# A two-layer diffusion step on one core: attention values in products of 512 columns, and layer 2's adaLN as a pass of its own

## The reference, cut to what matters

```python
def trunk_layer(x, cond, lp, ctx_kv, rope):
    mod = jax.nn.silu(cond) @ lp['w_ada'] + lp['b_ada']          # adaLN: (1024,) @ (1024, 6144)
    sh1, sc1, g1, sh2, sc2, g2 = jnp.split(mod[:, None, :], 6, axis=-1)
    h = rms_norm(x, lp['norm1']) * (1.0 + sc1) + sh1
    proj = h @ lp['w_in']                                        # gates, branches A, B and C
    ...
    o_lat = latent_attention(q_lat, q_pe, ckv, kpe)              # 8 heads, keys: own + 128 cached
    ...
    x = x + g1 * (merged @ lp['w_out'])
    h2 = rms_norm(x, lp['norm2']) * (1.0 + sc2) + sh2
    x = x + g2 * peer_ffn(h2, lp['peer_wq'], lp['peer_sub_keys'], lp['peer_u'], lp['peer_v'])

    # in latent_attention, per block of 128 queries:
    p = jax.nn.softmax(s, axis=-1)
    return jnp.einsum('bhqk,bkc->bqhc', p, ckv)                  # the values

    # in peer_ffn: each token picks 128 of 16384 experts (8 heads, 16 each)
    a = jax.nn.gelu(jnp.einsum('tkd,td->tk', jnp.take(u_tab, ib, axis=0), tb))
    return jnp.einsum('tk,tkd->td', gb * a, jnp.take(v_tab, ib, axis=0))
```

## Time and profile before

| | us |
|---|---|
| median of 3 runs (lowest, highest) | 5152.7 (5149.1, 5155.6) |
| the profiled execution's own time | 5154.9 |
| its span, first to last instruction | 5152.0 |

### The profile page before, as it was taken

How to read it: one execution, slowest core, us unless ns; L and a number is a source line. 1 busy time by engine, 2 the same in 40 slices (tenths; PEclk the granted TensorE clock), 3 DMA queues, 4 the chain that set the end, 5 groups by cost and what they waited for, 6 DMA issues and landing times.

```text
span 5152.0 us, 37623 instructions
## 1 busy us (share of the span) xinstructions
PE 4042.2 (78%) x11663; PEld 1906.6 (37%) x11663; DVE 3140.8 (61%) x7049; ACT 521.8 (10%) x1158; POOL 2525.1 (49%) x2570
## 2 busy tenths in 40 slices
PE   8889889893887777777788988989277777777777
PEld 4674543341323333333343545334122222222223
DVE  1155877667555665654554678766766666665553
ACT  1130320100001001000000224001000000000000
POOL 0003345403665665665565234550177676676674
PEclk9889999996998999999999989999699999999999
DMA  8536679718999998999998466993299999999997
GB/s 264 168 120 223 211 265 329 270 49 281 399 398 349 371 363 346 371 395 370 355 398 297 163 208 221 334 318 101 96 381 408 352 374 389 374 375 378 368 409 287
DMA packets 578101, 1562.80 MB, mean 303 GB/s; under 512 B 51104, under 2 KB 246256, under 8 KB 576626
## 3 DMA queue, kind: packets, MB, share of 16 engines
q0 software_dynamic: 368640, 1342.34, 68.8%
q1 hardware_dynamic: 208690, 217.90, 12.9%
q10 hardware_dynamic: 576, 0.16, 0.0%
HBM read 1557.44 MB, written 2.79 MB: 303 GB/s over the span
## 4 chain that ended last, share of the span: by engine, by line
PE 32%; DMA 31%; DVE 14%; POOL 13%; issue 7%; DVEq 2%; ACT 1%; SPq 0%; PEldq 0%; PEld 0%; POOLq 0%; ACTq 0%
DMA rows<-in_peer_u_dram,idx 15%; DMA rows<-in_peer_v_dram,idx 15%; POOL rows L2056 13%; PE ps L1213 10%; PE ps L757 5%; DVE rows L1941 4%; PE ps L1103 4%; PE ps L740 3%; DVE work L1983 2%; PE ps L767 1%; PE ps L802 1%; PE ps L1106 1%; DMA ring<-in_w_in_dram 1%; DVE work L1894 1%; PE ps L1007 1%
## 5 line engine op out<-in xcount | busy, mean ns | idle before, releaser
L1213 PE MATMUL ps<-rows,work 128*128 128x512 f32 x4096 | 2014.7, 625 | 662.3 <-DMA rows<-in_peer_v_dram,idx 616.0
L1941 DVE CUSTOM_DVE_ANT_0 rows<-rows,ps 128x1024 f32<-128x1024 f32 x1024 | 1248.7, 1220 | 1140.3 <-DMA rows<-in_peer_u_dram,idx 1129.1
L2056 POOL DMA_INDIRECT rows<-in_peer_u_dram,idx x1280 | 1252.9, 979 | 1336.7 <-DVE idx L1934 805.6
L2056 POOL DMA_INDIRECT rows<-in_peer_v_dram,idx x1280 | 1271.5, 993 | 1263.5 <-PE ps L1213 536.2
L1213 PEld LDWEIGHTS ps<-rows,work 128*128 128x128 f32 x4096 | 738.7, 196 | 1859.5 <-issue 1396.7
L757 PE MATMUL ps<-h_s,ring 128*128 128x512 f32 x1024 | 451.9, 596 | 3.8 <-DMA ring<-in_w_in_dram 3.8
L1941 DVE CUSTOM_DVE_ANT_0 rows<-rows,work 128x1024 f32<-128x1024 f32 x256 | 312.6, 1224 | 152.7 <-DMA rows<-in_peer_u_dram,idx 145.8
L2020 DVE TENSOR_SCALAR work<-cst,acts,g_w 128x128 f32<-128x128 f32 x1024 | 369.8, 363 | 37.6 <-PE ps L1213 22.6
L1983 DVE SCALAR_TENSOR_TENSOR work<-rows,acts,work 128x1024 f32<-128x1024 f32 x254 | 325.7, 1282 | 4.8
L757 PE MATMUL ps<-work,ring 128*128 128x512 f32 (+1 forms) x768 | 276.8, 515 | 59.7 <-DMA ring<-in_w_branch_c_dram 34.2
L757 PEld LDWEIGHTS ps<-h_s,ring 128*128 128x128 f32 x1024 | 196.4, 192 | 255.1 <-issue 250.4
(11 more groups left out here) (286 smaller groups left out, 3086.4 us busy)
## 6 DMA issues: line engine op xcount, KB each, us to landing
ring<-in_w_in_dram SPq DMA_DIRECT2D x72, 1024.0 KB, 11.4
ring<-in_w_ada_dram SPq DMA_DIRECT2D x48, 1024.0 KB, 7.7
ring<-in_peer_wq_dram SPq DMA_DIRECT2D x32, 1024.0 KB, 5.9
rows<-in_peer_u_dram,idx POOLq DMA_INDIRECT x1280, 7.3
rows<-in_peer_v_dram,idx POOLq DMA_INDIRECT x1280, 7.1
ring<-in_w_out_dram SPq DMA_DIRECT2D x16, 1024.0 KB, 12.2
ring<-in_tables_dram SPq DMA_DIRECT2D x10, 1024.0 KB, 8.0
ring<-in_w_branch_c_dram SPq DMA_DIRECT2D x16, 512.0 KB, 10.6
```

The lines of the kernel that those rows point to most:

```text
L1213: mm = pe.matmul(y_acc[:, cols], diag[:, e % TOPK, :], rows[:, ROWS + s, cols], start=e == 0, stop=e == EXPERTS - 1)
L1941: dve.tensor_tensor_reduce(rows[:, s, :], rows[:, s, :], tok, 1.0, 0.0, ALU.mult, ALU.add, dots[:, e:e + 1]).then_inc(rows_u_free, 1)
L2056: pool.indirect_dma_start(rows[:, slot0 + s, :], None, table, bass.IndirectOffsetOnAxis(ap=idx[:, t % 2, e:e + 1], axis=0)).then_inc(came[ ...
```

## The change

Two edits.

**adaLN.** A pass kind A is added: A0 stands ahead of P0, A1 between S0 and P1, each only the 24 products and copies. In `cuts` the steps of A1 get the slots -14 to 9, one each, and P1's remaining steps the slots 24 to 497. SyncE issues the 24 loads of w_ada ahead of the layer's parameter loads.

**Values.** The turned probabilities of a head's four query tiles are kept side by side (5 x 512), and the values of a head are 5 products of 512 columns, issued in steps 6, 10, ..., 34 right behind the scores. The probabilities have 2 buffers instead of 3. The buffer `work` grows by 640 columns.

The diff, without the shifted view offsets, the dispatch in the three `mixing` functions, and SyncE's `chunk_order` and `weights`, which move the 24 loads in the same way:

```diff
-INSTS = [INPUT, PROMPTS[0], SAMPLES[0], PROMPTS[1], SAMPLES[1]] + LASTS
+ADAS = [Inst("A", l) for l in range(LAYERS)]
+INSTS = [INPUT, ADAS[0], PROMPTS[0], SAMPLES[0], ADAS[1], PROMPTS[1], SAMPLES[1]] + LASTS
...
-VAL_LAG = 3
-STEPS = PAIRS + VAL_LAG + 2
+VAL_STEP = STILES + 2
+STEPS = PAIRS + 5
...
-        ring("params", ("turned", 0), ("turned", 1), *[("ada", n) for n in range(N_ADA)], "mod")
+        ring("params", ("turned", 0), ("turned", 1), "mod")
...
         if l + 1 < LAYERS:
-            pr = PROMPTS[l + 1]
-            steps = [(int(share * SPREAD * SAMPLE_SLOTS), place) for place, share in mix_share(pr)]
+            pr, ada = PROMPTS[l + 1], ADAS[l + 1]
+            steps = [(-PARTS + 1 + n, PLACE[ada, ("ada", n)]) for n in range(N_ADA)]
+            steps += [(N_ADA + int(share * (SPREAD * SAMPLE_SLOTS - N_ADA)), place) for place, share in mix_share(pr)]
...
+            def conditioning(i):
+                pe.wait_ge(cond_ready, 2)
+                for n in range(N_ADA):
+                    yield PLACE[i, ("ada", n)]
+                    w = arrived(i, ("ada", n))
+                    a = opened(i, ("ada", n))
+                    for k in range(KC):
+                        mm = pe.matmul(a[0:2, 0:CW], cond_t[:, 0:2, k], w[:, k, :], start=k == 0, stop=k == KC - 1)
+                    closed(i, ("ada", n), mm)
...
             for l in range(LAYERS):
+                weights(ADAS[l])
                 params(l)
...
+                    hv, past_step = divmod(m - VAL_STEP, STILES)
+                    if 0 <= hv < HEADS and past_step == 0:
+                        a = opened(i, ("V", hv))
+                        last_turn = hv * STILES + STILES - 1
+                        pe.wait_ge(*taken_at(i, ("Ta", last_turn)))
+                        pe.wait_ge(*taken_at(i, ("Tb", last_turn)))
+                        for b in range(TILES):
+                            lat = v.zc[:, b, Q_RANK:Q_RANK + KV_RANK] if b < STILES else past[:, 0, :]
+                            mm = pe.matmul(a[:, :], lat, v.prob_t[:, b, :], start=b == 0, stop=b == TILES - 1)
+                        closed(i, ("V", hv), mm)
                     t = m - 2
...
-                        for b in range(TILES):
-                            lat = v.zc[:, b, Q_RANK:Q_RANK + KV_RANK] if b < STILES else past[:, 0, :]
-                            mm = pe.matmul(v_bank[hv][:, jv * P:(jv + 1) * P], lat, v.prob_t[:, w % 2, b, :],
-                                           start=b == 0, stop=b == TILES - 1)
...
-                        took(act.copy(v.prob_t[:, t % 2, 0:STILES, :],
+                        cols = slice(t % STILES * P, (t % STILES + 1) * P)
+                        took(act.copy(v.prob_t[:, 0:STILES, cols],
```

More of the change, by code:

```diff
@@ L95, in step_turns @@
         turns.append((("Sa", m), m % 2))
+    if m >= VAL_STEP and (m - VAL_STEP) % STILES == 0 and (m - VAL_STEP) // STILES < HEADS:
+        turns.append((("V", (m - VAL_STEP) // STILES), 6))
     if 2 <= m < PAIRS + 2:
         turns += [(("Ta", m - 2), 3), (("Tb", m - 2), 4)]
-    v = m - VAL_LAG
-    if 0 <= v < PAIRS and v % STILES == 0:
-        turns.append((("V", v // STILES), 6))
     if m < PAIRS and m % STILES == 0:
@@ L121, in turn_order @@
         return o
+    if kind == "A":
+        ring(*[("ada", n) for n in range(N_ADA)])
+        return o
     if kind == "F":
@@ L209, in take @@
         o.append((name, slot, dmas, used))
-    if not i.sample:
+    if i.kind == "A":
         for n in range(N_ADA):
             take(("ada", n), ("full", ("ada", n)))
+        return o
     take("Q", ("full", ("qk", i.NT - 1)))
@@ L246, in chunk_table @@
     table, came, before, turn = {}, [0] * SLOTS, [None] * SLOTS, 0
-    for i in PROMPTS[:1] + SAMPLES[:1] + PROMPTS[1:] + SAMPLES[1:]:
+    for i in [i for i in INSTS if i.kind in "APS"]:
         for name, slot, dmas, used in chunk_order(i):
@@ L636, in weights @@
                 l = i.l
-                if not i.sample:
+                if i.kind == "A":
                     for n in range(N_ADA):
                         load(i, ("ada", n), cols_of(w_ada, l, n * CW))
+                    return
                 load(i, "Q", cols_of(w_in, l, COL_Q))
@@ L733, in parameters @@
                     closed(i, ("turned", n), mm)
-                pe.wait_ge(cond_ready, 2)
-                for n in range(N_ADA):
-                    yield PLACE[i, ("ada", n)]
-                    w = arrived(i, ("ada", n))
-                    a = opened(i, ("ada", n))
-                    for k in range(KC):
-                        mm = pe.matmul(a[0:2, 0:CW], cond_t[:, 0:2, k], w[:, k, :], start=k == 0, stop=k == KC - 1)
-                    closed(i, ("ada", n), mm)
                 yield PLACE[i, "mod"]
                 a = opened(i, "mod")
-                for n in range(N_ADA - RING_P, N_ADA):
-                    pe.wait_ge(*taken_at(i, ("ada", n)))
+                for n in range(N_ADA - 3, N_ADA):
+                    pe.wait_ge(*taken_at(ADAS[i.l], ("ada", n)))
                 for n in range(6 * KC):
-                    mm = pe.transpose(a[:, 2 * n:2 * n + 2], v.mod_rows[0:2, n * P:(n + 1) * P], ident[0:2, 0:2])
+                    mm = pe.transpose(a[:, 2 * n:2 * n + 2], mod_rows[0:2, n * P:(n + 1) * P], ident[0:2, 0:2])
                 closed(i, "mod", mm)
@@ L1284, in sine, with conditioning @@
                 act.activation(hid[0:HID, n, :], hid[0:HID, n, :], ACT.Sin).then_inc(sin_ready.sem, 1)
+            def conditioning(i):
+                for n in range(N_ADA):
+                    yield PLACE[i, ("ada", n)]
+                    a = full(i, ("ada", n))
+                    took(act.copy(mod_rows[0:2, n * CW:(n + 1) * CW], a[0:2, 0:CW]), i, ("ada", n))
             def mix(i):
@@ L1293, in mix @@
                 if not i.sample:
-                    for n in range(N_ADA):
-                        yield PLACE[i, ("ada", n)]
-                        a = full(i, ("ada", n))
-                        took(act.copy(v.mod_rows[0:2, n * CW:(n + 1) * CW], a[0:2, 0:CW]), i, ("ada", n))
                     yield PLACE[i, "mod"]
@@ L1431, in sample_attention @@
                         take_keys(h + 1, "Kb", SAMPLE, SAMPLE + PAST)
-                    w = m - VAL_LAG
-                    if 0 <= w < PAIRS and w % STILES == STILES - 1:
-                        a = full(i, ("V", w // STILES))
-                        took(act.copy(v.ol[:, w // STILES % 2, :], a[:, :]), i, ("V", w // STILES))
+                    hv, past_step = divmod(m - VAL_STEP, STILES)
+                    if 0 <= hv < HEADS and past_step == 0:
+                        a = full(i, ("V", hv))
+                        took(act.copy(v.ol[:, hv % 2, :], a[:, :]), i, ("V", hv))
                     if m >= 12 and m % 8 == 4:
@@ L1492, in mixing @@
                 for i in INSTS[1:]:
-                    yield from mix(i) if i.kind in "PS" else last_norm(i, LASTS.index(i))
+                    if i.kind == "A":
+                        yield from conditioning(i)
+                    else:
+                        yield from mix(i) if i.kind in "PS" else last_norm(i, LASTS.index(i))
             def soft(t, place):
@@ L1870, in mixing @@
                 for i in INSTS[1:]:
-                    yield from mix(i) if i.kind in "PS" else last_norm(i)
+                    if i.kind != "A":
+                        yield from mix(i) if i.kind in "PS" else last_norm(i)
             def select_part(t, part):
```

37 lines of the change are left out of this document (13 added, 24 removed).

## The result

| | before | after |
|---|---|---|
| median of 4 runs each, us | 5150.9 (5148.2 to 5155.6) | 5099.6 (5087.4 to 5106.8) |
| the profiled execution's own time (span) | 5154.9 (5152.0) | 5105.1 (5103.0) |

The ratio is 0.9905, with a 95% interval of 0.9889 to 0.9920. Run again beside other kernels it was 0.9903 (0.9885 to 0.9921). So the change takes 49 us off, where 24 were forecast. The sign was right, and the time is 2 us under the low end of the range.

The account below looks back on a forecast made before the run. The two expert gathers and their issue, 43% of the span, were taken to bound the kernel. 5154.9 - 21 + 1 - 4 = 5131 us for the profiled execution, 5129 as median; range 5102 to 5156.

Parts of the forecast that it names:

- Part 1: Layer 2's adaLN moved from beside layer 1's sample tiles into the selection: -21 us taken, bounds -50 to +3.
- P1's other work: Layer 1's tiles 2 to 4: 128.8 us extra time only moves, counted the same, 10 us either side.
- the stall: VectorE at layer 1's first diagonal, expert 18, waits for gelu behind last adaLN copies: 18.5 us, bounds 10 to 33.
- -43.3 + 18.5 + 3.5 + 1 = -20: Layer 1's first tile, us: 17 chunks no longer beside it, the stall, parameters beside gathers, later first dot product.
- Equal turns of the queues: Before the first diagonal, packet-by-packet turns would give adaLN's loads 73 GB/s: stall 25 us, Part 1 -14; not adopted.
- tile 1 ends at 1550 to 1565: Sign of a right forecast: layer 1's first sample tile ends then instead of at 1576.6 us.
- Part 2: Layer 1's start with A0: adaLN products end earlier, parameters are issued later; +1 us, bounds -3 to +5.
- Part 3: Attention's value products, 512 columns instead of 128: about -2 us a layer, -4 for both; bounds -24 and +14.
- Rival C: Attention's fourth step: value products ahead of Ta delay each head up to 3.1 us; slower, 5183, at half 5158; chance 0.08.
- A: Layer 1's first tile: no stall at expert 18, adaLN loads keep pace with the gathers; 5103 us, chance 0.17.
- B: Layer 1's first tile: saving given back, stall near 33 us or P1's work costing more there; 5144 to 5154, chance 0.23.

Follow-up runs that it names:

- 10: Changed kernel with the rest of P1 back at exactly the slots of the kernel before, layer 2's adaLN still in the selection; ratio 0.9949 to the kernel before.
- 3: Changed kernel with the rest of P1 from slot 140 on, some steps up to three slots later than in the kernel before; ratio 0.9908 to the kernel before.

## Why the prediction was right or wrong

The forecast for the sample tiles of layer 1 was -20 us. They gave -47.9: 6 us more by the terms of Part 1, and 22 us by a term that was put at nothing. The experiments cut it into three:

| step | from, to | us |
|---|---|---|
| adaLN out of tile 1, P1's slots kept | before to 10 | -26.1 |
| steps of P1 no longer ahead of a tile's sum | 10 to 3 | -17.0 |
| the rest of P1 from slot 24 and thinner (not resolved) | 3 to after | -4.8 |

**The failed step is "P1's other work (128.8 us of extra time in tiles 2 to 4) only moves, to 473 slots instead of 357; I count it the same, with 10 us to either side".** I took the 128.8 us for the cost of P1's work, to be carried along with it. In the changed kernel the same difference is 27.8 us in tile 1 (below) and 1198.8 - 1115.6 = 83.2 us in tiles 2 to 4, 111 us in all: 18 us less, outside my 10. 14 to 17 of them were no cost of the work, but of two places: steps that happened to stand ahead of a tile's sum on ScalarE. A shift by three slots in the one and by one slot in the other (10 to 3) was enough to remove both. It was to be read before the run: TensorE waited for the sum's copy 10.2 and 6.6 us in tiles 2 and 4, and 1.2 in tile 3 and at the end. I looked at the waits in tile 1 and in the attention, never in tiles 2 to 4, because I held that nothing of the change was in them. But P1's steps move there, and with them what stands ahead of a sum.

**Part 1, the selection and the stall: right.** Eight chunks by 1184.3 (forecast 1181.4), thirteen by 1203.6 (1200.8), the tokens turned by 1204.6 (1202.7), the first diagonal at 1269.3 (1267), idx to diagonal +18.1 us (+18.5, and 1 for the first dot product). From that diagonal to the end of tile 1, with P1's other work elsewhere, it is 282.8 us in run 10. The forecast was 284.8, layer 2's, and 3.5 for the parameters; these cost nothing that shows. So the terms -43.3 + 18.5 + 3.5 + 1 = -20 measured -26.1. One gap is left: with an eighth of adaLN's bytes the change was still worth 30.7 us of tile time, of which the last two rows of the table hold 21.8. Where the other 9 come from stays open; no run leaves out adaLN's products and copies beside tile 1.

**Equal turns of the queues.** The stall was 18.1 us, where Part 1 worked out 25 from the Trainium skill's rule of turns (DMA: Bandwidth & Descriptors, Queues, rings and completion order). Up to the first diagonal the ring moved 12.27 MB and the gathers 12.06 MB, with packets in the profile of 0.86 and 3.64 KB. If turns went by these packets, the ring would get a fifth of the bytes; it got half. That is against my working, but it doesn't test the rule: a packet in the Trainium skill's sense there bundles several descriptors, while the profile's packets are here about as large as one row (1 KB of a chunk, 4 KB of a table). I took the two for the same. How much each queue sends in a turn no run here shows, and the half is a mean over a stretch at whose end the gathers stood still.

**The marker "tile 1 ends at 1550 to 1565" was wrong by my own working.** I moved P1's work into 24 to 497 and forgot that a fifth of it then lies beside tile 1, where it costs 310.6 - 282.8 = 27.8 us. Tile 1 kept its length, and the saving showed up in tiles 2 to 4. Whoever compares the tiles alone, as I first did, looks for the cause in the wrong tile.

**Part 2, the start: +1 forecast, not resolved.** The row of idx gave +3.9 us, but the same code gave 392.7 to 403.0; the mean of the ten executions with A0 in the table is 398.3, that of the four without it 396.6. The steps were as forecast: the last adaLN product at 104.6 (104.1), the parameters' first use at 111.3 (109.9), after a wait of 6.7 us for them.

**Part 3, the values: -4 forecast; 4.6 us less measured alone, and 1 us beside the new adaLN,** both with intervals that hold nothing too. Rival C made the fourth step decide. Its wait came: ScalarE stood 23.2 us for Ta, in eight times, 2.9 us each, over the 2 us that I had named as its mark. Its price didn't, for the wait for the maxima fell by 19.2 us in the same stretch, and no run shows the stage longer.

**The rivals.** A gave nearly the time that came, 5103, but not for its reason: it had no stall, and there was one, as forecast. B (given back in the stall) falls with the first diagonal at 1269. That the result lies beyond the low end comes from a cost that no part of the range held: a bound of 10 us around a number that was one row of windows, and whose inside I hadn't opened.

## What to carry to other kernels

When the change moves work in a program whose order is fixed, the cost of the moved work isn't all its own. Before carrying a difference of windows along, list the waits inside it that happen only once or twice and are long: these can belong to a place in the order, and here a few slots decided them. On an engine that is 10% busy a step that waits 20 us is harmless until the one instruction that another engine needs stands behind it; put such hand-overs (a tile's sum, a bank's take) ahead of steps that may wait, and leave the taker the time that its record shows. To test such a wait, put it in on one side and take it out on the other. Here shifts of up to four slots were worth 14 to 17 us, and three slots more between the halves of six sums about 34.
